# State-space groups: skip term and gate applied chunk by chunk behind the outputs, their inputs loaded by chunk, and the sums of squares placed ahead of the state products

## The reference, cut to what matters

```python
o_b, ... = _bidir(_ssd_scan, (x_f, sb, sc, a_f), (x_b, sb, sc, a_b), init[2], init[3])
o_b = o_b + lp['d_skip'].reshape(SSM_GROUPS, SSM_HPG, 1) * xh          # skip term
o_b = o_b.reshape(Bn, L, SSM_INNER) * jax.nn.silu(z)                   # gate
o_b = rms_norm_3(o_b.reshape(Bn, L, SSM_GROUPS, SSM_INNER // SSM_GROUPS),
                 lp['ssm_norm_w'].reshape(SSM_GROUPS, SSM_INNER // SSM_GROUPS)).reshape(Bn, L, SSM_INNER)
y_b = o_b @ lp['w_pb']
merged = jax.nn.sigmoid(gate_a) * y_a + jax.nn.sigmoid(gate_b) * y_b
```

## Time and profile before

| | us |
|---|---|
| median of 3 runs | 3487.12 (3480.87 to 3489.39) |
| the profiled execution | 3491.64 |
| its span, in which the trace's times count | 3489.6 |
| PE busy | 3258.9 (93% of the span) |
| DVE busy | 2117.2 (61%) |
| ACT busy | 1249.0 (36%) |
| POOL busy | 1371.3 (39%) |
| this stage in the trace | 2712.7 to 3054.0 |

### The profile page before, as it was taken

One profiled execution on the slowest core, in us unless ns is written; L12 is line 12 of the kernel. 1 busy time (PEld: TensorE's weight loads), 2 busy tenths in 40 slices (PEclk: granted clock), 3 DMA queues, 4 the chain that ended last, 5 costly groups with the idle time before them and its releaser, 6 DMA issues. The chain is left out here.

```text
span 3489.6 us, 44690 instructions
## 1 busy us (share of the span) xinstructions
PE 3258.9 (93%) x17806; PEld 2622.1 (75%) x17806; DVE 2117.2 (61%) x2504; ACT 1249.0 (36%) x1899; POOL 1371.3 (39%) x625
## 2 busy tenths in 40 slices
PE   8999998999998998999999999888989868899998
PEld 6778777888866677977888877767877646678886
DVE  6586865889865476354756554868982777631112
ACT  4233343323344332333423342334441654332222
POOL 3434343444432233435344433326641322334443
PEclk9999999999999999999999999999999979999999
DMA  3223353465333245444444222533333755422322
GB/s 120 91 85 125 123 172 131 168 233 179 132 113 97 79 132 156 129 164 156 148 145 151 96 98 88 176 97 125 105 113 115 231 156 151 154 85 83 106 92 76
DMA packets 237662, 451.26 MB, mean 129 GB/s; under 512 B 59936, under 2 KB 120032, under 8 KB 230416
## 3 DMA queue, kind: packets, MB, share of 16 engines
q1 hardware_dynamic: 230384, 437.93, 38.8%
q10 hardware_dynamic: 7072, 10.49, 0.8%
HBM read 396.88 MB, written 51.46 MB: 128 GB/s over the span
## 5 line engine op out<-in xcount | busy, mean ns | idle before, releaser
L288 POOL TENSOR_TENSOR stream_feed_lo<-stream_feed_raw,stream_feed_hi 128x1024 fp32r<-128x1024 f32 (+4 forms) x555 | 1255.8, 2265 | 2013.4 <-ACT stream_feed_hi L281 1959.5
L281 ACT ACTIVATE stream_feed_hi<-stream_feed_raw 128x1024 fp32r<-128x1024 f32 (+4 forms) x555 | 533.3, 963 | 707.5 <-PE ffn_low L188 174.9
L186 PE MATMUL shared_ps<-third_h_hi,stream_feed_hi 128*128 128x512 f32 (+1 forms) x776 | 322.1, 415 | 39.2 <-ACT third_in_rows_bend L794 17.1
L187 PE MATMUL shared_ps<-third_h_lo,stream_feed_hi 128*128 128x512 f32 (+1 forms) x776 | 311.3, 401 | 0.0
L188 PE MATMUL shared_ps<-third_h_hi,stream_feed_lo 128*128 128x512 f32 (+1 forms) x776 | 311.3, 401 | 0.0
L186 PE MATMUL mixer_acc<-first_h_hi,stream_feed_hi 128*128 128x512 f32 x544 | 222.2, 408 | 7.2 <-DVE first_h_lo L1406 5.4
L480 DVE SCALAR_TENSOR_TENSOR ffn_ada_sum<-ffn_ada_w,cond,ffn_ada_sum 128x512 f32<-128x512 f32 x196 | 219.0, 1134 | 4.1
L186 PEld LDWEIGHTS shared_ps<-third_h_hi,stream_feed_hi 128*128 128x128 f32 (+1 forms) x776 | 151.1, 195 | 85.6 <-issue 44.3
L188 PE MATMUL mixer_acc<-first_h_hi,stream_feed_lo 128*128 128x512 f32 x544 | 214.2, 394 | 0.0
L187 PE MATMUL mixer_acc<-first_h_lo,stream_feed_hi 128*128 128x512 f32 x544 | 214.1, 394 | 0.0
L186 PE MATMUL ffn_low<-ffn_mid_hi,stream_feed_hi 128*128 128x512 f32 x528 | 207.6, 393 | 4.7 <-DVE x_res L702 4.6
(11 more groups left out here) (767 smaller groups left out, 7243.0 us busy)
## 6 DMA issues: line engine op xcount, KB each, us to landing
...
```

The source lines that it names most:

```text
L186: nc.tensor.matmul(out, w_hi, x_hi, start=start, stop=False)
L187: nc.tensor.matmul(out, w_hi, x_lo, start=False, stop=False)
L281: self.nc.scalar.activation(self.hi[:, p % self.cut, :n], self.raw[:, p % self.deep, :n], ACT.Copy).then_inc(self.cut_hi, 1)
L288: eng.tensor_tensor(self.lo[:, p % self.cut, :n], self.raw[:, p % self.deep, :n], self.hi[:, p % self.cut, :n].bitcast(F32), ALU.subtract) ...
```

## The change

Two things move. First, `gate` works by chunk instead of by tile: behind `out` of chunk `c` and the eviction there, it treats chunk `c - 1` with four skip instructions of 128 by 128 and one gate product of 128 by 4 by 128; the last chunk comes right behind the last `out`. The two places of `gate` in the next group's first part are gone. SP loads x and gate by chunk (128 by 4 by 128 elements, so that a run of consecutive bytes is 512 long, where it was 2,048) and at other places: chunks 0 and 1 where tiles 0 and 1 were loaded, chunk 2 behind `load_e` 6, and chunk 3 behind the next group's `load_start` and its first `load_e`; each waits for `gated`, so that its place is free. Second, ACT's `square` moves ahead of the next group's fourth `decay` and waits for the whole gate, and PE's `sums` moves from behind the second state product to ahead of the first one.

```diff
--- before.py
+++ after.py
@@ -3894,7 +3894,7 @@
         b_tok = s.sb("b_tok", [P, 4, P])
         xdt, xw = s.sb("xdt", [P, 2, 4, 512]), s.sb("xw", [P, 3, 512])
         cb, tri, tmp = s.sb("cb", [P, 2, 4, P]), s.sb("tri", [P, 2, P]), core.sumsq2
-        y, xg, z = s.sb("y", [P, 4, T]), s.sb("xg", [P, 2, T]), s.sb("z", [P, 2, T])
+        y, xg, z = s.sb("y", [P, 4, T]), s.sb("xg", [P, 2, 4, P]), s.sb("z", [P, 2, 4, P])
         w = s.sb("w", [P, 2, 4, 8])
         dense = Branches(nc, core, s, feed, h, ps, merged, dram["gates"])
         squares = (states[:, 0, 2], states[:, 1, 1], states[:, 0, 3], states[:, 1, 0])
@@ -3963,21 +3963,18 @@
                     sp.wait_ge(read, 8 * g + n - 2)
                     loads.load_e(sp, g, n)
 
-                def load_gate(g, j):
-                    n = 4 * g + j
+                def load_gate(g, c):
+                    n = 4 * g + c
                     if n >= 2:
                         sp.wait_ge(gated, n - 1)
-                    sp.dma_start(xg[:, j % 2], dram["xbc"][n * P:(n + 1) * P]).then_inc(xz_in[j % 2], 16)
-                    sp.dma_start(z[:, j % 2], dram["z"][Z3["z"] + n * P:Z3["z"] + (n + 1) * P]
-                                 ).then_inc(xz_in[j % 2], 16)
+                    for to, at in ((xg, dram["xbc"][T * g:T * (g + 1)]),
+                                   (z, dram["z"][Z3["z"] + T * g:Z3["z"] + T * (g + 1)])):
+                        sp.dma_start(to[:, c % 2], rows(at)[:, :, c * P:(c + 1) * P]).then_inc(xz_in[c % 2], 16)
 
                 for g in range(4):
                     dense.sync_gates(sp, pieces_by(g - 1, 1, 2) if g else 0)
                     dense.sync(sp, before(g, 0))
-                    if g:
-                        for j in range(2, 4):
-                            load_gate(g - 1, j)
-                    else:
+                    if g == 0:
                         load_x(0, 2)
                         load_x(0, 3)
                     for n in range(6, 8):
@@ -4004,6 +4001,7 @@
                     dense.sync(sp, pieces_by(g, 1, 0))
                     dense.sync_gates(sp, pieces_by(g, 1, 0))
                     load_e(g, 6)
+                    load_gate(g, 2)
                     for n in range(2, 4 if g < 3 else 0):
                         load_cum(g + 1, n)
                     load_e(g, 7)
@@ -4012,10 +4010,10 @@
                         for n in range(4, 6):
                             load_cum(g + 1, n)
                         load_start(g + 1)
-                        for n in range(3):
-                            load_e(g + 1, n)
-                for j in range(2, 4):
-                    load_gate(3, j)
+                        load_e(g + 1, 0)
+                    load_gate(g, 3)
+                    for n in range(1, 3 if g < 3 else 0):
+                        load_e(g + 1, n)
                 sp.wait_ge(intra_ready, 28)
                 sp.dma_start(core.x[:], dram["x_keep"]).then_inc(x_back, 16)
                 for q in range(2 * DT, 3 * DT):
@@ -4089,6 +4087,9 @@
                         if j == 1:
                             fill(g, 0, 1)
                     fill(g, 0, 2)
+                    if g:
+                        pe.wait_ge(x_scaled, 8 * g + 8)
+                        sums(g - 1)
                     for n in range(6):
                         d, c = n % 2, chunk(n)
                         pe.wait_ge(weighted, 6 * g + n + 1)
@@ -4100,8 +4101,6 @@
                             pe.wait_ge(advanced, 6 * g + n - 1)
                         nc.tensor.matmul(ps[:, 6 + d], b_tok[:, c], xw[:, n % 3], start=True, stop=True
                                          ).then_inc(product_, 1)
-                        if n == 1 and g:
-                            sums(g - 1)
                         if d:
                             fill(g, 0, 3 + n // 2)
                     for c in range(4):
@@ -4151,8 +4150,8 @@
 
                 def square(g):
                     act.wait_ge(inter_ready, 4 * g + 4)
+                    act.wait_ge(gated, 4 * g + 4)
                     for j in range(4):
-                        act.wait_ge(gated, 4 * g + j + 1)
                         a.activation(squares[j], y[:, j], ACT.Square).then_inc(squared, 1)
 
                 def root(g):
@@ -4180,11 +4179,11 @@
                     for n in range(2 if g == 0 else 0):
                         decay(0, n)
                     dense.scalar(act, before(g, 0))
+                    if g:
+                        square(g - 1)
                     for n in range(2 if g == 0 else 3, 4):
                         decay(g, n)
                     dense.scalar(act, pieces_by(g, 0, 0))
-                    if g:
-                        square(g - 1)
                     dense.scalar(act, pieces_by(g, 0, 1))
                     for n in range(4, 6):
                         decay(g, n)
@@ -4225,15 +4224,15 @@
                         v.tensor_tensor(h[1][:, n % DT], src, h[0][:, n % DT].bitcast(F32), ALU.subtract
                                         ).then_inc(dense.lesser, 1)
 
-                def gate(g, some):
-                    for j in some:
-                        n = 4 * g + j
-                        dve.wait_ge(y_made, 4 * g + 4)
-                        dve.wait_ge(xz_in[j % 2], 32 * (n // 2 + 1))
-                        v.scalar_tensor_tensor(out=y[:, j], in0=xg[:, j % 2], scalar=core.v("d_skip", n), in1=y[:, j],
-                                               op0=ALU.mult, op1=ALU.add).then_inc(skipped, 1)
-                        dve.wait_ge(skipped, n + 1)
-                        v.tensor_tensor(y[:, j], y[:, j], z[:, j % 2], ALU.mult).then_inc(gated, 1)
+                def gate(g, c):
+                    n, part = 4 * g + c, y[:, :, c * P:(c + 1) * P]
+                    dve.wait_ge(y_made, n + 1)
+                    dve.wait_ge(xz_in[c % 2], 32 * (n // 2 + 1))
+                    for j in range(4):
+                        v.scalar_tensor_tensor(out=part[:, j], in0=xg[:, c % 2, j], scalar=core.v("d_skip", 4 * g + j),
+                                               in1=part[:, j], op0=ALU.mult, op1=ALU.add).then_inc(skipped, 1)
+                    dve.wait_ge(skipped, 4 * n + 4)
+                    v.tensor_tensor(part, part, z[:, c % 2], ALU.mult).then_inc(gated, 1)
 
                 def invert(g):
                     dve.wait_ge(summed, g + 1)
@@ -4307,8 +4306,6 @@
                         v.tensor_tensor(w[:, d], edges[:, head(d, g), :].rearrange("p h c -> p c h"),
                                         cum_tok[:, :, head(d, g)], ALU.subtract).then_inc(w_diffed, 1)
                     dense.vector(dve, before(g, 0))
-                    if g:
-                        gate(g - 1, (0, 1))
                     dve.wait_ge(grammed, g + 1)
                     if g:
                         dve.wait_ge(masked[0], 4 * g)
@@ -4328,8 +4325,6 @@
                                             ).then_inc(x_scaled, 1)
                         if j == 1:
                             dense.vector(dve, pieces_by(g, 0, 0))
-                    if g:
-                        gate(g - 1, (2, 3))
                     dense.vector(dve, pieces_by(g, 0, 0))
                     dve.wait_ge(w_exped, g + 1)
                     dve.wait_ge(x_scaled, 8 * g + 8)
@@ -4357,8 +4352,10 @@
                             mask(g, c + 1)
                         out(g, c)
                         dense.vector(dve, before(g, 1) if c == 0 else pieces_by(g, 1, c - 1))
+                        if c:
+                            gate(g, c - 1)
+                    gate(g, 3)
                 dense.vector(dve, 2 * DT)
-                gate(3, range(4))
                 invert(3)
                 norm(3)
                 low_parts(DT + 12, 4)
```

## The result

The changed kernel takes 3508.45 us (median of 4 runs, 3504.09 to 3513.8) against 3487.78 for the kernel before beside it: a ratio of 1.006, interval 1.0047 to 1.0073, 20.7 us more, above the predicted range. The profiled execution took 3505.67 us (before 3491.64).

What follows compares the result with a forecast made beforehand. No engine is full; waits between DVE and PE at the group heads were taken to bound the kernel. Terms 3.5 + 5.5 - 0.1 - 0.5 = +8.4 us on 3487.12 gave 3495.5 us (+0.24%), range 3480 to 3506.

Steps and rivals of the forecast that it cites:

- the sums of squares: PE's sums ahead of the first state product: 3.60 us for eight records, priced +0.7 us in group 2, 0 in group 1.
- the 2.78 of gates already gone: Group 1 between xdt and weigh: 2.78 us of gates for tiles 2 and 3 vanish, counted within the +3.5 at weigh.
- the first rival: Chunk 3's loads are in time, so the gates gone give -6.7 us, 3480.4 in all; chance 0.15.
- The loads of the last chunk: Heads of groups: chunk 3's z lands late, at 2784.1 for group 1; xdt there 6.9 us late, weigh +3.5.
- 2775.1 + 0.5: SP in group 0: first load_e of the next group ends at 2775.1, plus 0.5 us for the second issue.
- neither costs by itself: SP's queue: decay differences and load_e 7 behind a wait for gated were said to add no cost.
- the 2.7: Queue cost of chunk 2's pair put in front: 2.7 us in 512-byte runs, against 1.6 in the old form.
- the four tiles of 2.5 us: Head of group 1: PE's four fill tiles, 12 matmuls, between the transposes, reckoned at 2.5 us.
- the tail: Behind the last out of group 3: predicted -0.5 us, bounds -3 and +1.5.
- spare time of DVE: Outputs: 1.2 us more gate time per group is covered there; without that cover it would cost 5 us.
- The queue backs up: Short runs cost over 2.7 us a pair, or chunks 0 and 1 delay others; +15.9 us, 3503; chance 0.20.
- Short runs are as fast as long ones: Pairs in 512-byte runs are each 1.1 us cheaper, 4.4 less at both heads; +4.0 us, 3491; chance 0.15.

Runs made afterwards that it cites:

- e4: Changed kernel with chunk 3's loads moved right behind the load of decay factor 7; 3497.07 us, ratio 1.0029 to the kernel before.
- e6: Changed kernel with chunk 3's loads right behind decay factor 7 and only PE's sums back behind the second state product; 3486.57 us, ratio 1.0 to the kernel before.
- e7: Changed kernel with chunk 3's loads right behind decay factor 7 and only ACT's squares back at their old place; 3491.82 us, ratio 1.0011 to the kernel before.
- e5: Changed kernel with chunk 3's loads right behind decay factor 7 and squares and sums at their old places; 3486.36 us, ratio 0.9995 to the kernel before.
- e13: Kernel before with one edit, PE's sums ahead of the first state product; gates, loads and squares as before; 3489.3 us, ratio 1.0 to the kernel before.
- e9: Changed kernel with the same bytes loaded at the same places in 2,048-byte instead of 512-byte runs; 3508.66 us, ratio 1.0052 to the kernel before.
- e3: Changed kernel without chunk 3's loads (its gate reads chunk 1's data) and with squares and sums at their old places; 3486.72 us, ratio 1.0 to the kernel before.

## Why the prediction was wrong

The direction and the chain were right: z late, `xdt` late, `weigh` close behind it, PE idle for an eviction, and the first skip's waits of 5.49, 5.05 and 4.84 us. The size was not.

*The step that failed is the one on the sums of squares*, "+0.7" in group 2 and "In group 1 I take 0" (with "I count nothing" for ACT and POOL beside it). In the changed kernel it is 3.8 us in group 2 and 1.6 in group 1 by the traces, together 4.7 above the price, of the 8.5 us by which the stage missed the sum. With the loads early, the place of the sums alone is worth 4.0 us in group 1 and 1.9 in group 2 (e4 against e6), and in the medians of the whole 10.5 us there and 5.5 between e7 and e5. In group 2 the duration was wrong: I took 3.60 us from a row in which PE ran at the full clock, behind products; at the new place the sums come out of 10.81 us of idling and take 6.61. In group 1 they took 3.60 as priced, and the path was wrong: `advance` now waits for the product behind them, 5.57 us where it waited 2.16.

And I counted "the 2.78 of gates already gone" as a gain, and did not ask what had run beside them. In the kernel before, with the gates, the sums' move costs nothing that can be told (e13). In its group 2 the rows show the sums running under the gates; in group 1 a wait for a decay factor takes up the 2.9 us. That the gates are the cover is read from these rows and not shown by a run: none has the sums in front and the gates back at their place in the changed kernel, and e13 has the old loads too.

*The gain of the gates that are gone* did not come either. With the loads in time I reckoned -6.7 us (the first rival). e4, where no wait for z is left, lies at +9.1; and with the sums back as well (e5, e6) the kernel takes the time of the one before.

*The loads of the last chunk.* Landing and `xdt` came out, 2782.24 + 2.12 = 2784.4 on the clock of the trace before against 2784.1, but by another way, and that they agree so closely is luck: z was issued at 2779.3 on that clock, 3.7 us behind the 2775.1 + 0.5 that I began with, not 2.7, and landed 5.0 us later, not 5.8. I had taken the last `out` of group 0 to be in time; it was 4.0 us late, 1.0 of it by the longer wait for decay factor 7, which "neither costs by itself" had left out, and most of the rest by the gates in the outputs. e9 refutes that pairs cost more because of their short runs, and with it the reason for the 2.7. In group 1 the four tiles of 2.5 us took 4.1, after idling and at a granted clock of 0.66; that is 1.6 of the 2.3 by which `weigh` missed. In group 2 the step to `weigh` was smaller than predicted, +3.3 for +4.8.

*Groups and tail.* A chunk took 1.8 us for 1.7 predicted, and the tail came out. That the gates inside the outputs run in spare time of DVE I had read from group 2 alone. It holds in groups 1 and 2 (i1 to o1 -0.5, i2 to o2 +0.7), not in group 0, as said, and not in group 3, where 2.5 us were lost, 1.9 of them in the outputs (i3 to o3); every run with these gates loses 1.5 to 4.4 us there. Only the sum over the groups comes to nothing (e3, e5).

*The rivals.* "The queue backs up", at 3503, was nearest, but by chance: its mark, z after 2786 in group 0, did not come (2784.4), and its upper bounds left out the sums. "Short runs are as fast as long ones" was right on the transfers: with runs of 2,048 bytes (e9) the time is that of the change with runs of 512. The Trainium skill (DMA: Bandwidth & Descriptors, Specifications) gives 512 bytes or more as the size for line rate, and e9 agrees. But the 4.4 us of this rival did not come, since the lateness was one of place.

What stays open: why e7 gains 5 us on e4 with squares alone back, beside sums in front (the points show 2.3 of them, made in the outputs of group 2 and in the tail); and whether the gates were the cover, as said. One reading of the rows was wrong without consequence: the granted clock of 0.85 is that of group 1, 0.79 that of group 2.
